# One program for the input projection, the rwkv mixer and the first steps of the ssd and gla mixers

## What is computed

```python
p = x @ w_in
s_z, s_xbc, s_dt, rw, gq, gk, gv, gg, ga = _split(p, IN_SPLITS_2)
# rwkv: every slice is mixed with the position before it
p = p + (prev - p) * mu
r, k, v, w_lr, a_lr, g_lr = _split(p, RWKV_SPLITS)
w = -softplus(-(w0 + tanh(w_lr) @ w2)) - 0.5;  decay = exp(-exp(w))
a = sigmoid(a0 + a_lr @ a2);  g = sigmoid(g_lr) @ g2
# per head (4 heads of 64), position by position:
state = state * w_t + sa[..., None] * (kk_t * a_t) + v_t[..., None] * k_t
y_t = state @ r_t
# ssd: a width-4 convolution and silu of xbc, softplus of dt, a decayed scan, times silu(z), norm
# gla: log_sigmoid(a_lr @ w_a2 + b_a) / 16, cumulated within chunks, a decayed scan, norm, times silu(g)
```

## Time and profile before

| what | value |
|---|---|
| median of three runs | 2203.06 us |
| the profiled execution | 2201.56 us, span 2200.3 us |
| mean granted clock of TensorE | 0.944 |
| TensorE busy | 1935.9 us, 88% |
| VectorE, ScalarE, GpSimd busy | 862.9, 655.4, 52.1 us |
| read from HBM | 536.73 MB, 244 GB/s over the span |

### The profile page before, as it was taken

One profiled execution on the slowest core, in us unless ns is written; L12 is line 12 of the kernel. 1 busy time (PEld: TensorE's weight loads), 2 busy tenths in 40 slices (PEclk: granted clock), 3 DMA queues, 4 the chain that ended last, 5 costly groups with the idle time before them and its releaser, 6 DMA issues. The chain is left out here.

```text
span 2200.3 us, 42423 instructions
## 1 busy us (share of the span) xinstructions
PE 1935.9 (88%) x18282; PEld 1350.2 (61%) x18282; DVE 862.9 (39%) x1731; ACT 655.4 (30%) x1203; POOL 52.1 (2%) x58
## 2 busy tenths in 40 slices
PE   7999999899969875789999999598768899999995
PEld 6899998799959643744444444296437444444432
DVE  5766667666656543421111111265434211111112
ACT  4554444544443331211111111233312111111111
POOL 0400002200000000000000000000000000000000
PEclk9999999999989987889999999899878899999998
DMA  6345552345524001599999999440015999999992
GB/s 254 116 137 189 192 188 97 134 159 186 173 81 154 1 2 62 224 381 427 427 429 429 429 428 427 167 154 1 2 49 226 382 427 427 428 429 429 428 427 115
DMA packets 48880, 540.07 MB, mean 245 GB/s; under 512 B 6192, under 2 KB 7376, under 8 KB 8144
## 3 DMA queue, kind: packets, MB, share of 16 engines
q1 hardware_dynamic: 48720, 537.80, 60.6%
HBM read 536.73 MB, written 1.05 MB: 244 GB/s over the span
## 5 line engine op out<-in xcount | busy, mean ns | idle before, releaser
L2491 PE MATMUL experts_psG<-weights_gu,experts_xc 128*64 128x512 f32 x2048 | 454.8, 593 | 19.4 <-DMA weights_gu<-in_moe_up 19.2
L2491 PEld LDWEIGHTS experts_psG<-weights_gu,experts_xc 128*64 128x64 f32 x2048 | 146.6, 137 | 316.3 <-issue 277.5
L409 DVE TENSOR_TENSOR ring_low<-ring_raw,ring_high 128x1024 fp32r<-128x1024 f32 x180 | 224.2, 1248 | 156.6 <-ACT ring_high L403 156.4
L403 ACT ACTIVATE ring_high<-ring_raw 128x1024 fp32r<-128x1024 f32 x180 | 189.1, 1054 | 155.9 <-PE ffn_ps L526 91.3
L2516 PE MATMUL experts_psD<-weights_d,experts_hT 128*64 128x512 f32 x1024 | 233.8, 598 | 1.6 <-ACT experts_hT L2452 1.6
L2422 DVE SCALAR_TENSOR_TENSOR experts_yc_low<-experts_psD,experts_slot_gate,experts_yc_high 128x512 fp32r<-128x512 f32 x64 | 48.0, 750 | 387.1 <-ACT experts_yc_high L2455 387.1
L524 PE MATMUL ffn_ps<-first_x_high,ring_high 128*128 128x256 f32 x704 | 198.4, 282 | 0.1
L525 PE MATMUL ffn_ps<-first_x_low,ring_high 128*128 128x256 f32 x704 | 198.0, 281 | 0.0
L526 PE MATMUL ffn_ps<-first_x_high,ring_low 128*128 128x256 f32 x704 | 197.9, 281 | 0.0
L2412 DVE TENSOR_TENSOR experts_sig<-experts_sig,experts_psG 128x256 f32<-128x256 f32 x64 | 26.9, 421 | 370.3 <-ACT experts_sig L2443 370.3
L2443 ACT ACTIVATE experts_sig<-experts_psG 128x256 f32<-128x256 f32 x64 | 24.6, 384 | 420.4 <-PE experts_psG L2491 420.4
(11 more groups left out here) (492 smaller groups left out, 3478.3 us busy)
## 6 DMA issues: line engine op xcount, KB each, us to landing
weights_gu<-in_moe_gate SPq DMA_DIRECT2D x64, 2048.0 KB, 25.3
weights_gu<-in_moe_up SPq DMA_DIRECT2D x64, 2048.0 KB, 29.8
weights_d<-in_moe_down SPq DMA_DIRECT2D x64, 2048.0 KB, 28.7
ring_raw<-in_w SPq DMA_DIRECT2D x90, 1024.0 KB, 4.9
project_w_raw<-in_w_in SPq DMA_DIRECT2D x22, 1024.0 KB, 5.0
output_w_raw<-in_w_out SPq DMA_DIRECT2D x8, 1024.0 KB, 7.8
project_w_raw<-in_w_in SPq DMA_DIRECT2D x2, 1056.0 KB, 4.9
const<-in_const SPq DMA_DIRECT2D x1, 1344.0 KB, 17.4
```

What stands on the lines that cost most here:

```text
L403: act.activation(self.high[:, n % AHEAD], self.raw_half(n), ACT.Copy).then_inc(self.rounded, 1)
L409: dve.tensor_tensor(self.low[:, n % AHEAD], self.raw_half(n), self.high[:, n % AHEAD], ALU.subtract)\
L2491: ins = pe.matmul(out, xc[:, kk], wgu[:, place, kk, :, j * S:(j + 1) * S], start=kk == 0, stop=kk == DT - 1)
```

## The change

`stage_project2` and `stage_rwkv` are replaced by one stage, `stage_mix2`; `stage_ssd_gla` keeps its place behind them and begins at the products of cx. `Units` takes the place of `Stream` there: a unit is one tile (512 KB), `tokm` is two halves over the contraction, 24 units in all, 4 raw and 4 split places. The order of units is LOW (the low-rank inputs of rwkv), K0, K1, R0, R1, V0, V1, GA, GQ, GK, GG0, GG1, TOKA, TOKB, X0 to X5, Z0 to Z3. Every engine's list is now: for each unit its own step for it, then `after(u)`, a piece of the chains. Banks 6 and 7 of PSUM alternate for the tiles; the chains use 0 to 5. The factors share memory with the unshifted rw, and several other tiles of rwkv share places. Units 0 and 1 are rounded between the squares and the Ln of the norm and split between centring and scaling; units 2 and 3 behind the splits of x. `idle_products` and its tile are removed everywhere. The sets of ScalarE's function tables are loaded by name. The bf16 parts of x for the experts (`parts`) are allocated inside the loop. On the host the columns of `w_in2` are laid in the order of the units.

```diff
+class Units:
+    def load(self, sp, i, src):
+        if i >= self.slots:
+            sp.wait_ge(self.split, i - self.slots + 1)
+        sp.dma_start(self.raw[:, i % self.slots, 0:self.sizes[i]], src).then_inc(self.loaded[i % self.slots], 16)
+    def round(self, act, i):
+        act.wait_ge(self.loaded[i % self.slots], 16 * (i // self.slots + 1))
+        if i >= self.n2:
+            act.wait_ge(self.used, i - self.n2 + 1)
...
+LOW, K0, K1, R0, R1, V0, V1_, GA, GQ, GK, GG0, GG1, TOKA, TOKB, X0, Z0 = list(range(15)) + [20]
+UNIT_SIZES = [DT * P] * 12 + [DT * N_TOKM // 2] * 2 + [DT * P] * 10
...
             @block.vector
+                n_vec(dve, ch, first_rests)
+                xs.rest(dve, k.x)
+                for i in range(2, 4):
+                    w.rest(dve, i)
+                for u in range(N_UNITS):
+                    w.rest(dve, u + 4)
+                    after(u)
...
+                    elif u == R1:
+                        shift(u)
...
+                        dve.scalar_tensor_tensor(F[:, A_], kk[:], -1.0, ex[:, 2], ALU.mult, ALU.mult).then_inc(F_ready, 1)
+                        dve.tensor_tensor(F[:, B_], rk[:], ex[:, 1], ALU.mult).then_inc(F_ready, 1)
+                    elif u == V0:
+                        shift(u)
+                        dve.tensor_tensor(F[:, K_], k_, ex[:, 1], ALU.mult).then_inc(F_ready, 1)
+                    elif u == GG1:
+                        inverse(0)
+                    elif u == TOKA:
+                        inverse(1)
+                    elif u == X0:
+                        inverse(2)
+                    elif u == X0 + 1:
+                        inverse(3)
+                        convolve((0, 1))
+                    elif u == X0 + 2:
...
+                    elif u == X0 + 3:
+                        convolve((2, 3))
+                    elif u == X0 + 4:
...
+                    elif u == X0 + 5:
+                        convolve((4, 5))
+                    elif u == Z0 + 1:
+                        state(1)
+                        state(2)
...
             @block.scalar
+                n_act(act, first_rounds)
+                xs.round(act, k.x, normed)
+                for i in range(2, 4):
+                    w.round(act, i)
+                act.preload_act_table_set("sigmoid_and_others")
+                for u in range(N_UNITS):
+                    act.wait_ge(w.used, u + 1)
+                    if u == TOKB:
+                        act.activation(b.tokm[:], ps[:, 4:6, 0:N_TOKM], ACT.Copy).then_inc(tokm_copied, 1)
+                    elif u != TOKA:
+                        act.activation(dst(u), ps[:, bank(u), 0:S], ACT.Copy).then_inc(copied, 1)
+                    w.round(act, u + 4)
+                    after(u)
...
+                    elif u == GK:
+                        powers(0)
+                    elif u == GG1:
+                        powers(1)
+                    elif u == TOKA:
+                        powers(2)
+                    elif u == X0:
+                        powers(3)
+                    elif u == Z0 + 3:
+                        act.wait_ge(copied, in_turn(u) + 1)
+                        act.activation(sz, b.z[:], ACT.Sigmoid).then_inc(z_sig, 1)
+                        act.preload_act_table_set("natural_log_exp_and_others")
...
             @block.tensor
+                def after(u):
+                    if u == K1:
+                        pe.wait_ge(lact_ready, 3)
...
+                    elif u == R0:
+                        pe.wait_ge(kksq_ready, 1)
+                        heads64(3, t1, ones64).then_inc(low_done, 1)
+                    elif u == V1_:
+                        pe.wait_ge(F_ready, 2)
+                        products(0, A_, B_)
+                        products(1, B_, A_)
+                        pe.wait_ge(F_ready, 3)
+                        products(2, K_, A_)
+                    elif u == GA:
+                        transposes(0, F[:, A_])
+                        transposes(1, F[:, B_])
+                    elif u == GQ:
...
+                        pe.wait_ge(masked, 3)
+                        squares(0)
+                    elif u == GK:
...
+                    elif u == GG0:
+                        squares(1)
+                        inverse(0)
+                    elif u == GG1:
+                        squares(2)
+                        inverse(1)
...
+                    elif u == TOKB:
+                        squares(3)
+                        inverse(2)
+                    elif u == X0:
+                        inverse(3)
+                    elif u == X0 + 1:
+                        pe.wait_ge(inv_updated, 4)
...
+                    elif u == X0 + 3:
+                        states_and_ends()
+                    elif u == X0 + 5:
+                        read_out()
+                    elif u == Z0:
+                        state(1)
+                    elif u == Z0 + 1:
+                        state(3)
+                    elif u == Z0 + 2:
+                        state(5)
...
+                            if kc == DT // 2 and u > Z0:
+                                state(2 * (u - Z0))
...
+                state(NCH - 1).then_inc(inter_done, 1)
+                pe.wait_ge(yy_ready, 1)
+                heads64(4, yy, k.c("centre64")).then_inc(centred, 1)
+                pe.wait_ge(sq_ready, 1)
+                heads64(3, sq, ones64).then_inc(var_done, 1)
...
-                act.activation(sg[:], cx[:], ACT.Sigmoid).then_inc(sig_ready, 1)
...
-                idle_products(pe, b, psD[:, 1], 12)
-                pe.wait_ge(x_ready, 1)
...
-                stage_project2(nc, k, L, a["w_in2"], a["vec2"], a["ln2"], a["lr2"], vecs, b)
-                stage_ssd_gla(nc, k, vecs, b, a["wa2"], L, b.y)
-                stage_rwkv(nc, k, vecs, b, L, b.y)
+                stage_mix2(nc, k, L, a["w_in2"], a["vec2"], a["ln2"], a["lr2"], a["wa2"], vecs, b, b.y)
+                stage_ssd_gla(nc, k, vecs, b, b.y)
```

More of the change, by code:

```diff
@@ L190, in vector @@
             dve.wait_ge(centered, DT)
+        if between is not None:
+            between()
         dve.wait_ge(rstd_ready, 1)
@@ L1270, in _ @@
+                act.wait_ge(centred, 1)
+                act.activation(flat(sq[:]), ps[:, 4], ACT.Square).then_inc(sq_ready, 1)
+                act.wait_ge(var_done, 1)
+                ch.link(act.activation(flat(lnv[:]), ps[:, 3], ACT.Ln, bias=k.eps[64e-5], scale=1.0 / 64))
+                act.activation(rstd[:], lnv[:], ACT.Exp, scale=-0.5).then_inc(rstd_ready, 1)
             @block.tensor
             def _(pe):
[L1272 to L1285 removed]
@@ new lines, in products @@
+                def products(i, a, c):
+                    bank, off = 2 * (i // 3), (i % 3) * P
+                    for n in range(NP):
+                        pr, blk = n // SB, n % SB
+                        for j in range(CPB):
+                            cols = slice(blk * P + C * j, blk * P + C * (j + 1))
+                            for g in range(2):
+                                rows = slice(64 * g, 64 * g + 64)
+                                ins = pe.matmul(ps[C * j:C * (j + 1), bank + g, off + n * C:off + (n + 1) * C],
+                                                F[rows, a, pr, cols], F[rows, c, pr, cols], start=True, stop=True,
+                                                tile_position=(64 * g, C * j))
+                    ins.then_inc(masked_done, 1)
@@ new lines, in _ @@
+                n_pe(pe)
+                for u in range(N_UNITS):
+                    w.ready(pe, u)
+                    if u in (TOKA, TOKB):
+                        if u == TOKA:
+                            pe.wait_ge(tok_copied, 4)
+                        half = DT // 2
+                        weights = w.weights(u, half)
+                        for blk in range(SB):
+                            (sh, sl), out = xs.block(blk), ps[:, 4 + blk, 0:N_TOKM]
+                            for i in range(half):
+                                kc = i + (half if u == TOKB else 0)
+                                pe.matmul(out, sh(kc), weights[0][:, i], start=kc == 0, stop=False)
+                                pe.matmul(out, sh(kc), weights[1][:, i], start=False, stop=False)
+                                ins = pe.matmul(out, sl(kc), weights[0][:, i], start=False, stop=kc == DT - 1)
+                    else:
+                        if in_turn(u) >= 2:
+                            pe.wait_ge(copied, in_turn(u) - 1)
+                        high, low = w.weights(u, DT)
+                        out = ps[:, bank(u), 0:S]
+                        for kc in range(DT):
+                            if u == 0:
+                                pe.wait_ge(xs.split, kc + 1)
+                            if kc == DT // 2 and u > Z0:
+                                state(2 * (u - Z0))
+                            pe.matmul(out, high[:, kc], xs.high[:, kc], start=kc == 0, stop=False)
```

(7 more changed lines are left out.)

968 lines of the change are left out of this document (474 added, 494 removed).

## The result

The changed kernel takes 2150.14 us, median of 4 runs (2146.89 to 2155.80), beside 2203.95 (2199.18 to 2205.13) for the kernel before on the same chip: ratio 0.9763, 95% interval 0.9737 to 0.9788. Forecast: 2138, range 2106 to 2175. Its profiled execution took 2149.94 us (span 2148.6), 51.7 less span than before, where 65 were forecast.

A forecast was written before the change was run, and what follows sets the result against it. The prediction took the projection as bound by TensorE, the stretches behind it by chains of short steps. Gains of 19.1+12.4+0.9 = 32.4 us per layer, 65 for two, gave 2138 us, range 2106 to 2175.

The forecast's parts named there:

- Entry: Norm and first splits, up to the first projection product: 22.3 us where the kernel before takes 25.1.
- Products, pieces, clock: TensorE in the new stage: projection tiles 71.1 us, rwkv's small products 27.5, loss at 1.2 GHz 5.
- Waits: TensorE waiting in the new stage for chain steps that the written order puts late: 18.5 us.
- Fetch: Instruction-packet stalls of TensorE within the larger pieces of rwkv: two of 2.2 us, 4.5 us.
- Tail: New stage from the last state product to its end: 8.5 us, where it was 7.4.
- Stage: Entry, projection and rwkv as one stage: 157.4 us against 176.5, a gain of 19.1 per layer.
- ssd and gla: Stage behind the new one: G products 3.0 us in, no table load, a gain of 12.4 us per layer.
- Output: Output projection's start: first transfer issued earlier, with fewer semaphores to clear, a gain of 0.9 us per layer.
- Rival 1: New stage: each piece above 64 products stalls once on fetch, 22 us per layer; 2173 us, chance 0.14.
- Rival 2: TensorE-bound throughout: waits 9 us, no fetch or clock loss, no loss in ssd; 2096 us, chance 0.12.
- Rival 3: Lock step: every piece waits for its own unit, 24 us more waits per layer; 2202 us, chance 0.05.
- Rival 4: Clock stays at 1.2 GHz in the new stage and ssd, 27 us slower per layer; 2257 us, chance 0.07.

The follow-up runs named there:

- kernel with the steps ahead: Changed kernel with nine awaited chain steps issued ahead of the unit's own copy, rounding or split: 2123.63 us, ratio 0.9637 to the kernel before.
- bursts: Changed kernel with 1024 small products of zeros ahead of the last norm, alone (2202.45 us) or with a 512-column product after every eighth (2260.70 us).
- early output weights: Changed kernel with the output projection's four weight loads issued at the start of ssd and gla, into their own buffer: 2139.29 us, ratio 0.9708.
- kernel with both changes: Changed kernel with awaited steps issued first, output weights loaded from the start of ssd and gla, their first unit split there: 2105.40 us, ratio 0.9573.
- The burst: Changed kernel with 1024 small 32 x 32 products of zeros issued back to back ahead of the last norm: 2202.45 us, ratio 1.0006 to the kernel before.
- mixed burst: Changed kernel with 1024 small products of zeros ahead of the last norm and a 512-column product after every eighth: 2260.70 us, ratio 1.0279.
- doubled products: Changed kernel with each of rwkv's 160 factor products issued twice: 2170.57 us, ratio 0.9863 to the kernel before.

## Why the prediction was right, and where it was off

Forecast against measured, first layer. The waits that the forecast names and those of the trace are compared one by one.

- *Entry:* 22.3 forecast, 22.3 measured.
- *Products, pieces, clock:* 71.1 + 27.5 + 5 = 103.6 forecast, 109.4 busy. These are the mis-sized terms. Each product counted up to the start of the next, the tiles take 78.8 us for 76.1 with the 5 for the clock, the pieces 30.6 for 27.5. TensorE ran at 1.2 GHz for 20.4 us of the stage (27.2 in the second layer), 17.1 of them behind the start, where 10 were forecast. At the prediction's 0.44 us lost per us that is some 3 of the missing 5.8. The clock fell behind the waits of V1, GG1, X0 and X5 (in the second layer behind X1 too), where the prediction had V1, X0 and X1. The second layer's stage is 3.8 us longer than the first's, 3.2 of them busy time at a clock of 0.90 for 0.92.
- *Waits:* V1 6 forecast, 4.8 measured; GG1 2 and 1.9; X0 and X1 6 and 6.1; X5 2.5 and 2.2; the rest 2 and 1.0. In all 18.5 forecast, 16.0 measured. The kernel with the steps ahead shows that those of GG1, X0, X1 and X5 were the order's.
- *Fetch:* 4.5 forecast, about 5 measured as "issue". The bursts show that packets can stall such pieces; that each of these stalls is one is inferred. The count of 128 was of records, which the prediction calls products.
- *Tail:* 8.5 forecast, 7.9 measured.
- *Stage:* 157.4 forecast, 160.7 measured. That it is so near is partly luck: 2.5 us less of waits and 0.6 less of tail stand against 5.8 more of busy time.
- *ssd and gla:* 43.0 forecast, 41 measured. VectorE's G products start at 800.65, 3.0 us behind the stage's last step at 797.7 as forecast, and there is no table load at the end.
- *Output:* 0.9 gain forecast, 0.2 measured. The transfers were issued 0.9 us earlier, as forecast, but the first had come only 5.7 us after its issue, where before it took 4.9.
- *Outside:* 0 forecast, 3.4 us lost behind the first output product (1.9 and 1.5), most of it in the experts (453.2 us from their first product to their last in the first layer, 451.5 before). It can't be told from these runs why. TensorE was at 1.2 GHz for 9.4 us of them where before had 3.4. With early output weights it was for 3.5, and they took 452.0; but the kernel with both changes has early weights too, and 8.8 and 452.8. So the clock goes with about one microsecond, is not shown to cause it, and does not come of the early weights.
- *The sum itself:* the 1.0 us of the barrier is counted in the 176.5 of the stage and stands once more in the 55.4 of ssd and gla, so the terms give 31.4 us per layer against the 241.85 of the earlier trace rows, and not 32.4. Measured were 29.2 and 25.5; the second layer's stage was not forecast apart.

Rival 1 (each longer piece stalls): the burst shows the mechanism, but the stage has some 5 us of "issue" and not 22. That packets come under the tiles between would explain it; the mixed burst and the doubled products fit that in part. Rival 2 falls with X0 and X1. Rival 3 (lock step) is refuted by the waits that are absent at the other units. Rival 4 (the clock stays at 1.2 GHz) did not happen: granted clock 0.92 and 0.87. The Trainium skill (TensorE: Matmul & The Clock Gate, A second HAM failure mode: psum-queue depth-cycling) tells of a clock that swings between its two levels where short idles stand between groups of products, not of one that stays low. The new stage shows such a swing, four times in the first layer behind the start, at a cost of a few us; the prediction drew too much from the section when it gave it rival 4's time.

## What to carry to other kernels

Where chains of short steps are woven between tiles of a busy engine, issue the step that another engine waits for ahead of this unit's own copy and split; on the same instructions that took 10 and 13 us off a stage of 135 and 139. Count small products as instruction packets (here 3.7 us for 128 records with their loads) before counting their columns, and put wide tiles that are needed anyway between them. And look for a transfer that stands open between two stages (11 us here, before as after): it can be issued, and its first unit prepared, in the stage before.

## What was not expected of the hardware

- A run of small f32 products and wide bf16 products of zeros, with one pause of 1.6 us at its start, stayed at 1.2 GHz for 118 us; during the norm's products of 256 columns behind it the clock went to 2.4 GHz.
- The clock of ssd came out as 0.89 or 0.81 for the same code, with 35.2 or 38.3 us, in one execution with the unchanged stage of after ahead of it.
- Raising the granted clock of ssd from 0.89 to 0.95 by fillers did not shorten it (35.5 and 35.4 us).
- Doubling 160 small products in the kernel before cost 13.3 us per layer where their packets alone account for 9.2.
